# Column order of the split matrix products: turns of two columns from two halves instead of straight through

## The reference, cut to what matters

```python
h = h + dsa_attention(h, a_norm_w, a_w_in, ..., a_w_out)        # q, k, v, indexer; top 64 keys per query
u = rms_norm(h, ffn_norm_w[0])
h = h + (silu(u @ w_gate) * (u @ w_up)) @ w_down                # dense, 2816 wide
k_sb, v_sb = split(rms_norm(h, kv_norm_w) @ kv_w)
h = h + stick_breaking_attention(h, b_norm_w, b_w_q, b_w_out, k_sb, v_sb)
u = rms_norm(h, ffn_norm_w[1])
h = h + moe_ffn(u, router_w, w_gate_up, w_down)                 # 8 experts, 2 per token
```

## Time and profile before

| | us |
|---|---|
| median of 3 runs | 1118.95 (1118.8 to 1119.88) |
| the profiled execution's own time | 1117.47 |
| its span, first to last instruction | 1115.6 |
| PE busy in the span | 1104.4 |
| granted TensorE clock over the span | 1.000 of full speed |

### The profile page before, as it was taken

One profiled execution on the slowest core, in us unless ns is written; L12 is line 12 of the kernel. 1 busy time (PEld: TensorE's weight loads), 2 busy tenths in 40 slices (PEclk: granted clock), 3 DMA queues, 4 the chain that ended last, 5 costly groups with the idle time before them and its releaser, 6 DMA issues.

```text
span 1115.6 us, 26142 instructions
## 1 busy us (share of the span) xinstructions
PE 1104.4 (99%) x11948; PEld 845.4 (76%) x11948; DVE 306.3 (27%) x438; ACT 253.5 (23%) x376; POOL 27.8 (2%) x71
## 2 busy tenths in 40 slices
PE   9999999999999999999999999999999999999998
PEld 7768999999899874567776776777677877677665
DVE  4785645555565341100100100110110100100112
ACT  4775534334536632000000000000000000000000
POOL 0000000000000004000000000000000000000000
PEclk9999999999999999999999999999999999999999
DMA  9639999766055179999999999999999999999982
GB/s 338 217 124 308 319 342 310 240 217 212 29 198 218 57 277 416 401 417 417 399 416 416 398 417 416 398 416 416 397 418 416 398 416 416 402 412 416 415 352 93
DMA packets 101805, 370.98 MB, mean 333 GB/s; under 512 B 6392, under 2 KB 36128, under 8 KB 90432
## 3 DMA queue, kind: packets, MB, share of 16 engines
q1 hardware_dynamic: 92368, 343.78, 78.7%
q0 software_dynamic: 5184, 19.92, 5.3%
q10 hardware_dynamic: 4144, 5.59, 1.4%
HBM read 347.65 MB, written 21.63 MB: 331 GB/s over the span
## 4 chain that ended last, share of the span: by engine, by line
PE 95%; DVE 2%; ACT 1%; DMA 0%; issue 0%; ACTq 0%; DVEq 0%
PE e_ps L924 41%; PE pair L924 20%; PE pair L522 9%; PE pair L523 9%; PE pair L524 9%; PE pair L558 1%; PE pair L584 1%; DMA norm_rows<-in_b_norm_w 0%; DVE up_lo L1554 0%; PE pair L623 0%; DVE dn_ring L1659 0%; PE pair L917 0%; ACT up_hi L1055 0%; PE pair L860 0%; PE pair L812 0%
## 5 line engine op out<-in xcount | busy, mean ns | idle before, releaser
L924 PE MATMUL e_ps<-e_ring,work 128*32 128x384 f32 (+1 forms) x6144 | 482.3, 459 | 0.0
L924 PEld LDWEIGHTS e_ps<-e_ring,work 128*32 128x32 f32 x6144 | 317.9, 110 | 131.3 <-issue 18.7
L924 PE MATMUL pair<-dn_ring,e_mem 128*32 128x256 f32 (+1 forms) x2016 | 162.9, 450 | 0.0
L924 PEld LDWEIGHTS pair<-dn_ring,e_mem 128*32 128x32 f32 x2016 | 107.0, 110 | 45.2
L1554 DVE TENSOR_TENSOR up_lo<-up_ring,up_hi 128x2048 fp32r<-128x2048 f32 x46 | 105.3, 2291 | 113.1 <-ACT up_hi L1055 113.0
L522 PE MATMUL pair<-uT_hi,up_hi 128*128 128x256 f32 x480 | 135.6, 282 | 0.8 <-DVE uT_lo L1568 0.6
L523 PE MATMUL pair<-uT_lo,up_hi 128*128 128x256 f32 x480 | 134.8, 281 | 0.0
L524 PE MATMUL pair<-uT_hi,up_lo 128*128 128x256 f32 x480 | 134.8, 281 | 0.0
L1055 ACT ACTIVATE up_hi<-up_ring 128x2048 fp32r<-128x2048 f32 x46 | 87.9, 1913 | 101.8 <-PE pair L524 97.0
L1370 ACT ACTIVATE e_mem<-e_ps 128x1152 f32<-128x1152 f32 (+1 forms) x16 | 16.8, 1050 | 361.3 <-PE e_ps L924 361.3
L924 PE MATMUL pair<-dn_more,e_mem 128*32 128x256 f32 (+1 forms) x1152 | 92.4, 450 | 0.0
(11 more groups left out here) (294 smaller groups left out, 786.9 us busy)
## 6 DMA issues: line engine op xcount, KB each, us to landing
e_ring<-in_moe_w_gate_up SPq DMA_DIRECT2D x64, 1536.0 KB, 20.8
e_ring<-in_moe_w_gate_up SPq DMA_DIRECT2D x64, 1280.0 KB, 17.6
dn_ring<-in_moe_w_down SPq DMA_DIRECT2D x56, 1024.0 KB, 19.4
dn_more<-in_moe_w_down SPq DMA_DIRECT2D x32, 1024.0 KB, 19.7
up_ring<-in_dense_w_gate_up SPq DMA_DIRECT2D x22, 1024.0 KB, 10.3
dn_ring<-in_dense_w_down SPq DMA_DIRECT2D x11, 1024.0 KB, 13.2
up_ring<-in_kv_w SPq DMA_DIRECT2D x4, 2048.0 KB, 8.6
x_rows<-q_T POOLq DMA_DIRECT2D x10, 768.0 KB, 7.2
```

The lines of the kernel that those rows point to most:

```text
L924: return pe.matmul(out, a, w, start=start, stop=stop, tile_position=(0, THIRD * place), skip_group_check=True)
```

## The change

The view that `product` gives to the matmuls is rearranged. The moving operand (both parts) and the sums are each seen as two halves, and the columns are taken as two from the first half, two from the second half, the next two from the first, and so on. For 256 columns the order is 0, 1, 128, 129, 2, 3, 130, 131, ...; for 512 columns it is 0, 1, 256, 257, 2, 3, .... Sum column c is still made from moving column c, and each matmul has as many columns as before. The number of instructions, the stationary operands, the waits, the increments and all DMAs stay as they are. All split products go through `product`, so all are changed; float32 matmuls are not.

```diff
+            def in_turns(v):
+
+                return v.rearrange("p (half c w) -> p c half w", half=2, w=2)
+
             def product(ps, a_hi, a_lo, b_hi, b_lo, start, stop, shared=False):
 
+                ps, b_hi, b_lo = in_turns(ps), in_turns(b_hi), in_turns(b_lo)
                 pe.matmul(ps, a_hi, b_hi, start=start, stop=False, skip_group_check=shared)
                 pe.matmul(ps, a_hi, b_lo, start=False, stop=False, skip_group_check=shared)
                 return pe.matmul(ps, a_lo, b_hi, start=False, stop=stop, skip_group_check=shared)
```

## The result

The changed kernel takes 1247.98 us (median of 4 runs, 1247.23 to 1248.47) beside 1118.88 us for the kernel before on the same chip: 129.1 us more, a ratio of 1.115 with a 95% interval of 1.1135 to 1.1165. The forecast was 1095.5 us, faster, with a range of 1092 to 1146; the time lies beyond it, between rivals D (1143.5) and C (1387). In the changed file the three matmuls of `product` stand in lines 527 to 529 and the experts' in line 929.

A forecast was written before the change was run, and what follows sets the result against it. PE was taken as the bound, busy 1104.4 of 1115.6 us. Gains of 13.4 and 11.3 us, less 0.8 and 0.4, gave 23.5 us off 1118.95: 1095.5 us, range 1092 to 1146.

The forecast's parts named there:

- D: Rival, split matmuls: lost cycles come with each stretch opened, turns open twice as many; +24.7 us, 1143.5 us; chance 0.14.
- C: Rival, split matmuls: each jump costs, rate falls to two cycles a column; +268 us, 1387 us; chance 0.20.
- Is there anything to gain or lose in a matmul?: Step on split matmuls: one cycle in about 13 is lost to neighbouring columns; alternation removes it, 9 and 17 ns a matmul.
- rows 8: Profile rows on expert matmuls: 48 records of 320 columns in 3.23 us, read as 4.8 columns a nanosecond against 2.2.
- (1): Split products: 1440 matmuls of 256 columns go from 118.3 to 109 ns, -13.4 us.
- (2): Split products: 648 matmuls of 512 columns go from 233.4 to 216 ns, -11.3 us.
- Term (3): First attention: about 48 matmuls of 512 columns lie under ACT and DVE; 0.8 us come back as waiting.
- Term (4): Split products: a few pieces begin behind a wait for a remainder; 0.4 us deducted.
- The covers: Slack under a faster PE: a microsecond for splitting in the row of eight pieces, 11 us for expert weights.
- B: Rival, split matmuls: address order does not matter, lost cycle belongs to float32r words; nothing changes, 1119 us; chance 0.20.

The follow-up runs named there:

- e1: Kernel before plus 21 groups of 12 extra matmuls in various column orders and data types; total meaningless; straight 229 ns a matmul, turns of two 339.
- e5: Kernel before plus 38 groups of 12 extra float32r matmuls, only the moving columns' read order varied; total meaningless; straight 229 ns, most turns of two 327 to 328.
- e4: Kernel before with the down-projection's sums written in turns of two, moving operand read straight; 1117.37 us beside 1117.55, ratio 0.9996.
- e9: Kernel before with the down-projection alone taking even pairs of columns first, then odd pairs, both sides; 1175.20 us beside 1117.44, ratio 1.0516.
- e8: Kernel before plus groups of 12 extra matmuls, sums straight, read orders varied; total meaningless; two fixed pairs 219 ns, two advancing pairs 328.

## Why the prediction was wrong

**The step that failed** is the one in "Is there anything to gain or lose in a matmul?": "I take it that neighbours get in each other's way once in 13 cycles, and that alternation removes it." The runs show the opposite, and the times fit one picture (an opening is a word for what they suggest; no view shows a fetch). Four neighbours of float32r, aligned, come in one opening, and leaving them after two makes a second opening necessary. In e1 512 columns that use each four once take 227 to 234 ns (straight, where the starts settle at 227 ns after the group's first few, and even fours then odd fours), and those that open each twice with others in between take 451. That is 1.77 ns for each of 128 openings in the one case and 1.76 for each of 256 in the other. Four columns at one a cycle need 1.67 ns. So a steady 1.77 ns an opening would explain the lost cycle of the straight stream too: bfloat16, which finds twice the columns in the same bytes, settles at 216, and orders that meet half as many new fours or none in the same 512 columns (e5, lines 916, 960, 964) take 218. That the straight loss is this fetch is an argument from these numbers; no run changed the fetch itself.

**The evidence from rows 8** was misread, twice. The 48 records are 24 matmuls: the float32 groups of e1 leave two records for each matmul (lines 950 and 952), and `expert_up` issues 24 for a tile. Counted by matmul the four streams pass 2.4 columns a nanosecond together, hardly more than the split product's 2.2. They pass 4.8 only if each record reads all its columns anew, which no run shows. And each of the four reads its own runs of 64 columns, at two cycles a column in a record, and leaves no four half used. The row could show at most that the memories serve four streams, not that one stream gains by changing places. The earlier trace rows had the same fault the other way: line 792 made its one jump in the sums and read a run of 128 columns twice. It could say nothing of short turns on the reading side, and the chance given to C and D together, 0.34, was too low for a form that no row showed.

**Terms (1) and (2)** had the right counts and the wrong sign: +48.4 ns instead of -9 and +93.5 instead of -17. The excess scales with columns, as the prediction said, and is indifferent to DMA (166.7 ns at a share of 0.86 and of 0.47), to the weight loads (e5, 32 stationary columns) and to which of the two shapes it is.

**Term (3)**, 0.8 us hidden under ACT and DVE in the first attention, hardly shows in this direction. The only waits of PE for DVE at that place, before the change, are these two, and the changed kernel has the second alone:

```profile
PE pair L614 <- DVE u L1603: 0.4, 1, 0.4
...
PE pair L614 <- DVE work L1603: 0.2, 1, 0.2
```

So about 0.4 us of the loss can have been hidden there, less than the differences between 130.3 us by matmul prices, 130.8 of PE's busy time and 130.5 between the spans can tell.

**Term (4)** supposed 0.4 us more of waiting for remainders with a faster PE. With a slower one the two longest such waits stayed at 1.1 and 0.6 us, and a third, 0.4 us, is gone.

**The covers** in the earlier trace rows were not put to the test, since PE became slower. ACT waited longer instead: 4.69 and 6.03 us before its two splits in the row of eight pieces that were looked at, where the earlier trace rows have 2.73 and 3.87.

**The rivals.** B's observation, that the lost cycle belongs to float32r words and not to the array, is right in that bfloat16 and repeated columns lose none, but its conclusion that order does not matter is not. C named the right mechanism in its first half ("the stream fetches a stretch of several columns at a time and uses only two of it"), and its second half, sums that are read, added and written back out of rhythm, is refuted by e4. Its price was too high: two cycles a column were assumed and one and a half measured. (Its limit for a turn of four, "4 x 0.455 = 1.85 ns", comes to 1.82; nothing hangs on it.) e9 shows an order that costs more than C's step, 452 ns against 430; the turns escape it because part of what was opened is still held at the second visit (two fixed pairs in turn, e8, cost nothing); that it is held is argued from these times. Had first visits cost 1.77 ns and second ones 0.83, eight columns would take 5.2 ns and 512 of them 333, near the 327 to 340 measured, and bfloat16 in turns, with 64 first visits and 192 later ones, would take 273, near its 271. That is a fit and not a finding: the same picture missed four of the groups of e8, and for turns of four it gives 227 where 251 was measured. D's doubling of the excess (251 ns) is what turns of four cost, by another way, not turns of two.

**The pages weighed.** The Trainium skill, PSUM — Partial Sum Buffer, Specifications (TRN2), has any non-contiguous pattern slow matmuls significantly; e4 and the groups with sums in turns or hops show no slowing at pairs, which fill that page's line of 8 bytes (0.9996, and 229 and 228 ns against 229). No run took sums one by one. The page pointed to the right side of the forecast for the wrong memory. The Trainium skill, SBUF — State Buffer (Door 1: The DMA port swizzle), has lines of 16 bytes, which the aligned turns of four in e1 and the misaligned ones in e8 bear out (251 and 331 ns), and asks for two hits on a line for full bandwidth; with exactly two successive hits on each line e1 measured 452 ns against 229, so for this operand the measurement decides against it.

**What stays open:** how many openings are held and in what order they are dropped; why eight repeated columns are free and four fixed pairs at four places cost 574 ns; why turns of whole aligned fours (251) cost more than the same fours read even first, odd after (233); and why one order, turns of two columns 256 apart, took 338 to 340 ns in e1 and at e5's lines 982 and 986 but 327 to 328 at e5's line 928, e8's line 918 and in the real kernel. No order tried in float32r, among those that read 512 different columns, was faster than straight reading, so there is no better version to offer from this study.

## What to carry to other kernels

Read the moving operand of a one-pass float32r matmul in whole, aligned groups of four columns, best straight through; half a group a visit, with the other half fetched after a jump elsewhere, cost 40% (turns of two) to 94% (e9) of the matmul here. Bfloat16 pays too: 25% in turns of two (e1). Sums could be scattered in pairs for nothing in e1 and e4, so where an order must be changed, store the operand in the wanted order and scatter the sums. And before forecasting a stride, ask whether any row has that run length on that side: a row with long runs, or with the jump on the other operand, is no evidence.

## What the runs showed of the hardware that was not expected

The reading and the summing side differ sharply: the same turns of two cost 340 ns on the moving operand and 229, the straight price, on the sums. A second place only four columns behind the first makes a matmul of 512 columns faster (218) than straight reading (229), though it reads only 260 different columns, while eight columns behind it costs 327. One group, two fixed aligned fours in turn (e8, line 924), took about 426 ns for its first five matmuls and 219 for the last six; no cause was looked for.
